# Gathered expert inputs: eight PSUM results over four banks in turn in place of two

## The reference, cut to what matters

```python
logits = jnp.einsum('btd,de->bte', h, P['moe_router'][i], preferred_element_type=jnp.float32)
probs = jax.nn.softmax(logits, axis=-1)
top_p, top_i = lax.top_k(probs, TOP_K)
top_p = top_p / jnp.sum(top_p, axis=-1, keepdims=True)
gate = jnp.sum(jax.nn.one_hot(top_i, N_EXPERTS, dtype=jnp.float32) * top_p[..., None], axis=-2)
hg = jnp.einsum('btd,edf->btef', h, P['moe_w_gate'][i])
hu = jnp.einsum('btd,edf->btef', h, P['moe_w_up'][i])
a = jax.nn.silu(hg) * hu * gate[..., None].astype(h.dtype)
return jnp.einsum('btef,efd->btd', a, P['moe_w_down'][i])
```

## Time and profile before

| | us |
|---|---|
| median of 3 runs | 1951.61 |
| lowest and highest of them | 1945.2, 1957.02 |
| profiled execution: its own time | 1947.83 |
| its span, first to last instruction | 1946.0 |
| TensorE busy in the span | 1863.8 (96%) |
| TensorE's mean granted clock | 0.979 of full speed |

### The profile page before, as it was taken

The page is one execution under the profiler, slowest core; times in us unless marked ns, Lnnn a source line. Parts: engine busy times, 40 slices in busy tenths (PEclk is TensorE's granted clock), DMA queues, the critical chain, the costliest instruction groups (busy, mean ns, idle before and its releaser), DMA issues.

```text
span 1946.0 us, 28135 instructions
## 1 busy us (share of the span) xinstructions
PE 1863.8 (96%) x11949; PEld 1293.0 (66%) x11949; DVE 519.7 (27%) x1150; ACT 366.1 (19%) x754; POOL 135.2 (7%) x226
## 2 busy tenths in 40 slices
PE   8999999899899999999999989989699999999998
PEld 5889878786678888788888868747433343433434
DVE  3453532428320000143544243533400000000000
ACT  2231334322010000015124432310110000100101
POOL 3000001203100000000100020320000000000000
PEclk9999999899999999999999989999889999899999
DMA  9842789989489876899759988996629999589993
GB/s 279 260 134 90 264 303 340 305 308 341 149 278 364 300 294 248 309 336 364 265 180 333 320 314 289 361 390 233 239 74 369 368 384 405 217 294 386 373 408 119
DMA packets 254691, 563.84 MB, mean 290 GB/s; under 512 B 11949, under 2 KB 149393, under 8 KB 254288
## 3 DMA queue, kind: packets, MB, share of 16 engines
q1 hardware_dynamic: 235232, 500.14, 71.8%
q0 software_dynamic: 18544, 58.58, 8.9%
q10 hardware_dynamic: 784, 3.25, 0.4%
HBM read 547.74 MB, written 196.63 MB: 383 GB/s over the span
## 4 chain that ended last, share of the span: by engine, by line
PE 91%; DMA 4%; DVE 2%; issue 1%; ACT 1%; POOL 0%; DVEq 0%; ACTq 0%; POOLq 0%
PE PS L866 30%; PE PS L1412 15%; PE PS L793 8%; PE PS L1438 7%; PE PS L1273 4%; PE PS L1313 4%; PE PS L786 3%; PE PS L1287 3%; PE PS L1374 3%; PE PS L910 2%; PE PS L903 2%; DMA arena<-bias_tables 1%; PE PS L1460 1%; PE PS L1244 1%; DMA arena<-in_cache_win_kv 1%
## 5 line engine op out<-in xcount | busy, mean ns | idle before, releaser
L866 PE MATMUL PS<-h,ring 128*128 128x264 f32 x2816 | 653.6, 389 | 0.0
L866 PEld LDWEIGHTS PS<-h,ring 128*128 128x128 f32 x2816 | 527.4, 190 | 106.5 <-issue 21.3
L1577 ACT COPY z<-PS 128x264 f32<-128x264 f32 (+3 forms) x307 | 130.7, 445 | 874.6 <-PE PS L866 527.0
L1412 PE MATMUL PS<-ring,z 128*32 128x512 f32 (+1 forms) x1440 | 212.2, 527 | 1.2 <-ACT z L1577 1.2
L1412 PE MATMUL PS<-arena,z 128*32 128x512 f32 (+1 forms) x1056 | 190.1, 535 | 0.0
L1412 PEld LDWEIGHTS PS<-ring,z 128*32 128x32 f32 x1440 | 68.5, 111 | 126.9 <-issue 111.4
L793 PE MATMUL PS<-h,ring 128*128 128x264 f32 x512 | 115.3, 386 | 1.6 <-DVE h L1965 1.6
L793 PEld LDWEIGHTS PS<-h,ring 128*128 128x128 f32 x512 | 97.2, 190 | 18.6 <-issue 2.0
L1438 PE MATMUL PS<-arena,z 128*32 128x512 f32 x432 | 104.0, 593 | 0.0
L1412 PEld LDWEIGHTS PS<-arena,z 128*32 128x32 f32 x1056 | 55.0, 110 | 53.5 <-issue 53.4
L1273 PE MATMUL PS<-z,ring 128*128 128x264 f32 x384 | 87.3, 388 | 0.0
(11 more groups left out here) (319 smaller groups left out, 1832.3 us busy)
## 6 DMA issues: line engine op xcount, KB each, us to landing
out_win_s<-in_cache_win_kv SPq DMA_DIRECT2D x128, 1023.5 KB, 10.0
ring<-in_w_in SPq DMA_DIRECT2D x88, 1024.0 KB, 6.3
out_win_s<-in_cache_win_kv SPq DMA_DIRECT2D x32, 1022.0 KB, 12.8
ring<-in_moe_w_gate SPq DMA_DIRECT2D x28, 1024.0 KB, 9.2
arena<-in_moe_w_up SPq DMA_DIRECT2D x22, 1024.0 KB, 11.5
ring<-in_moe_w_up SPq DMA_DIRECT2D x22, 1024.0 KB, 8.7
ring<-in_moe_w_down SPq DMA_DIRECT2D x20, 1024.0 KB, 11.3
arena<-in_moe_w_down SPq DMA_DIRECT2D x18, 1024.0 KB, 10.4
```

What stands on the lines that cost most here:

```text
L866: last = mm(bank(l, "p", j)[:, 0:T], w[:, k, P * (j % 2):P * (j % 2) + P], h[:, k, :], start=(k == 0), stop=(k == KT - 1))
L1412: last = mm(m_bank("c", "gu", g, b, w, r)[BLK * j:BLK * j + BLK, 0:n], hs[:, k, P * r + BLK * j:P * r + BLK * j + BLK], v3(slot_ap(set_slo ...
L1577: return nc.scalar.copy(out, in_)
```

## The change

The bank of `gh` job `d` is 2, 3, 0, 1, 2, 3, 0, 1 for `d` = 0 to 7, in both groups, in place of 2, 3, 2, 3, 2, 3, 2, 3. No instruction of arithmetic, no transfer and no order of work is changed; the waits and signals of these jobs go to the semaphores of the banks that they now use.

```diff
         def chosen_jobs():
-            out = [(("gh", 0, d), 2 + d % 2) for d in range(KT)]
+            out = [(("gh", 0, d), (2, 3, 0, 1)[d % 4]) for d in range(KT)]
             for g in range(2):
...
                 if g == 0:
-                    out += [(("gh", 1, d), 2 + d % 2) for d in range(KT)]
+                    out += [(("gh", 1, d), (2, 3, 0, 1)[d % 4]) for d in range(KT)]
                 out += [(("fd", g, d), 4 + d % 4) for d in range(KT)]
```

## The result

The changed kernel takes 1938.27 us (median of 6 runs, 1936.66 to 1939.98), the kernel before 1953.22 (6 runs, 1945.2 to 1957.02): a ratio of 0.9926, 95% interval 0.9905 to 0.9948, some 14 us less. In a later measurement on another occasion it was 0.9952 (0.9933 to 0.9970), some 9 us. The forecast of a gain of 13.3 us lies between the two. A gain in us that stands beside a ratio is worked out from the ratio; the difference of the medians is up to 3 us from it.

A forecast was written before the change was run, and what follows sets the result against it. TensorE has work in flight for 96% of the span, so time comes only from its waits or low clock. Gather 1's 7.2, gather 0's 5.2 and hidden 0's 0.9 make 13.3 us: 1951.6 to 1938.3, own range 1933 to 1944.

The forecast's parts named there:

- the cover that was forecast: In the gathers, each pair's wait for earlier copies has some 3.7 us of cover, one pair's duration less the copies.
- The rival that the change does nothing: Pairs in the gathers wait for something else too, the 0.66 us waits stay, same time as before; chance 0.04.
- A pair of 4.26 us, gather 1 of 17.04: Gather 1: four pairs without waits at the high clock, 17.04 in place of 24.22 us, 7.2 us saved.
- Gather 0: Gather 0: clock still rises in pair 2 at 1418.9; hidden 0 starts at 1430.4, not 1435.64, 5.2 us saved.
- The start of hidden 0: After gather 0's last pair: the wait for all eight copies stays, clock loss regained between 0 and 1.7 us, 0.9 taken.
- The weights followed: Weight sets after gather 1: requests wait for TensorE, so later sets are asked for earlier by as much as TensorE is early.
- Only the bare waits go: Both gathers: the clock still falls without waits, gain 4.4 us, time 1947.2 us; chance 0.17, shared with few falls gone.
- Given back to the weights: Hidden and down: transfers set the pace, an earlier start ends in waits for sets, 1951.6 us, no change; chance 0.05.
- The clock stays low through the gather: Both gathers: too little full-row work to hold or regain the high clock, a low pair 8.0 us, 1963 us; chance 0.04.

The follow-up runs named there:

- waits put back: Changed kernel with four banks, but each pair also waits until the results of the pair before it are copied; 1.0006 (0.9983 to 1.0029) of the kernel before.
- the filler: Kernel before, two banks, with an unused full-row result computed into bank 0 ahead of each wait of pairs 2 to 4; 0.9964 (0.9946 to 0.9983).
- gather 0 alone: Four banks in gather 0 only, gather 1 keeping the two of the kernel before; 0.9951 (0.9930 to 0.9972) of the kernel before.
- gather 1 alone: Four banks in gather 1 only, gather 0 keeping the two of the kernel before; 0.9961 (0.9941 to 0.9980) of the kernel before.
- the reordered blocks: Kernel before, two banks and all six waits, with the token blocks in a pair ordered full, 8, full rows; 1.0011 (0.9987 to 1.0035).

## Why the prediction was right, step by step

- **No cover was missing.** Pairs 2 to 4 wait for nothing in either gather; TensorE's waits for ScalarE inside the gathers are gone from the view. The copies of pair 1 end 3.7 us before pair 3 starts (1670.46, 1674.14), the cover that was forecast. The rival that the change does nothing fell with that.
- **A pair of 4.26 us, gather 1 of 17.04.** Gather 1 takes 17.04 us (1665.62 to 1682.66), to 0.01 us in all four profiles with four banks there and no waits put back. The step also had the split right: 2.2 us of waits and 5.0 of clock, against 2.1 and 5.1 with the filler. But 7.2 us is what the first profile of before gave; in the two later ones gather 1 had only one fall, and the gain would be 3.8 us (20.84 − 17.04). The price of a wait is 0.73 us always and 1.7 us sometimes.
- **Gather 0 was undersized.** I had left the clock's rise in pair 2, so that it took 26.6 us. It took 24.24 us (1412.43 to 1436.68) and 23.25 in the second profile, though a pause for issue inside pair 1 was 3.34 us in the first in place of 1.88: the clock rose before pair 1 was done, at 1420.9. But four more profiles with unfilled waits in gather 0 and the old order took 28.6 to 31.0 us in place of 31.85, in two of which the clock also rose in pair 1, so that the gain over a usual execution, some 5 to 7 us, is near the 5.2 of the sum. Its two errors, a late rise and a long execution to measure against, partly cancelled; that is luck.
- **The start of hidden 0.** I took the middle of 0 and 1.7 us. The clock did not fall there in the three profiles that have four banks in gather 0, no waits in it and the wait ahead of hidden 0 (changed kernel twice, gather 0 alone); it did in the three profiles of before, at some 1.7 us, with gather 1 alone and with the waits put back. With the reordered blocks it stayed up in the two executions that reached hidden 0 with it high. From the first matmul of hidden 0 to gather 1 it is 228.94 us after, 230.64 before. It is not safe: with the filler it did fall, though the last pair and the wait behind it are the same there.
- **The weights followed.** The first set after gather 1 was issued at 1704.91 in place of 1712.76, and from the first matmul of hidden 1 to the end it took 244.65 us (1693.53 to 1938.2) as before (244.66). Nothing was given back.
- **The size of the whole.** Sized by the profile, 7.6 + 1.7 + 7.2 = 16.5 us went in the three places, yet the two profiled executions differ by 7.9. The rest lies ahead of the change: gather 0 starts at 1412.43 after and 1403.79 before, 8.6 us later. Part of it is one wait near 955 us for the delta-rule blocks (L910 for VectorE), 8.9 us long in place of 3.4, in code that both kernels share; in the eleven other profiles of all variants it is 3.5 to 5.1 us, and gather 0 starts between 1407.6 and 1412.1. So one execution was early and the other as late as any. The sum was not hurt by it, because it used durations inside the stage and not its place.
- **How much of the hit was luck.** From the first matmul of gather 0 to the end, the three profiles of before take 542.2, 535.8 and 535.5 us, the two of the changed kernel 525.8 and 524.7. So the change is worth some 10 to 17 us, by when the clock rises in gather 0 and by how many falls an execution of before has: five in the gathers in the first, three in each of the others. The forecast took the one profile it had as the rule and set its gain off against a median of three runs. The mechanism was right; that 1938.3 us was forecast and 1938.27 measured is in part luck, and the later measurement has 9 us where the sum has 13.3.
- **The rivals.** "Only the bare waits go" fell (gather 1 takes 17.04 us at a clock of 1.00, not the 22 us of that rival). "Given back to the weights" fell. "The clock stays low through the gather" did not happen here, but its mechanism is real: it is what the reordered kernel did in gather 0, at 40.0 us, where a low pair took 9.3 us with its wait (1431.14 to 1440.42), that is 8.6 without it; I had priced it at 8.0.

The Trainium skill, "TensorE: Matmul & The Clock Gate", section "A second HAM failure mode: psum-queue depth-cycling", agrees with what the filler and the waits put back show: short idle times between groups that cycle through PSUM banks cost clock as well as time, if not at every wait. The same page's example in "HAM oscillation — how this bites in real kernels", where PSUM double-buffering gave no further gain once the loop was dense, is another case than this one: here more banks took away waits, and gave 0.9926 and 0.9952.

## What to carry to other kernels

A short wait for a PSUM bank can cost more than its length: price it by the duration of the same matmuls behind it and without it, and read the granted clock of the stretch that follows. Give successive results enough banks that a reader's copy ends while the next result is computed, and where no bank is free, even useless matmuls in the wait can pay (0.9964 here). Before you trust one profile on a clock effect, look at several executions: the falls, and the rise at the start of a stage, came and went between them.

## What the runs showed of the hardware that was not expected

- The reordered kernel, three executions: gather 0 took 26.7, 28.1 and 40.0 us. In the first two the clock was up from pair 2 on, in the third it stayed low through the whole gather, which cost 12.4 us.
- Falls behind equal waits vary: three of three in gather 1 in the first profile of before, one of three in each of the two later ones.
- The four-bank kernel was also steadier, as far as its fewer runs tell: its 12 timed runs in two measurements span 6 us (1936.7 to 1942.7), 50 of the kernel before in two measurements 17 us (1942.9 to 1959.4), in two clusters with mean clocks of 0.977 to 0.984 and 0.973 to 0.977.
